# Up products of the gated feed-forward: high and low tokens in one 512-column product, halves added on VectorE, first tap and gate product on GpSimd

## The chip, the cores and the metric

One core of one Trainium2 chip runs the whole program: a four-layer network on 256 tokens of width 1024, all in float32. The metric is the device time of one execution in microseconds, the median of several runs. Before the change it is 1380.42 us (three runs, 1379.06 to 1381.10).

## The reference, cut to what matters

Two mixture-of-experts layers come first, then two layers (2 and 3 in the kernel) whose feed-forward part is this:

```python
def conv_ffn(h, w_in, conv_w, conv_b, w_out):
    """Gated MLP: up-projection -> causal depthwise conv (width 3) -> SiLU gate -> down-projection."""
    u = h @ w_in
    C = u.shape[-1]
    u = lax.conv_general_dilated(u, conv_w[:, None, :], window_strides=(1,),
                                 padding=[(CONV_WIDTH - 1, 0)],
                                 dimension_numbers=('NWC', 'WIO', 'NWC'),
                                 feature_group_count=C) + conv_b
    a, b = jnp.split(u, 2, axis=-1)
    return (jax.nn.silu(a) * b) @ w_out
```

`h` is 256 x 1024, `w_in` 1024 x 5632, so a and b have 2816 columns each, and `w_out` is 2816 x 1024. For each column, token t gets `w2*u[t] + w1*u[t-1] + w0*u[t-2] + bias`.

## The kernel before, in words

**Precision by parts.** TensorE takes the rounded type float32r. A float32 matrix is split into a high part, rounded by a copy (ScalarE, `copy`, line 793), and a low part, the raw value less the high one (VectorE). A product is three: high weights by high tokens, high weights by low tokens, low weights by high tokens, summed in one PSUM bank. `split_product` (lines 1857 to 1859) does these three for each of 8 k-blocks of 128 rows, each a 128x128 weight load and a product of 256 columns (the tokens).

**Steps and blocks.** The up projection runs in 11 steps of 256 columns of a and 256 of b. A step has two blocks (c = 0, 1) of 128 columns of a (ab = 0) and of b (ab = 1). Steps are called j = 0, 1 within five turns (four turns in a hardware loop, the fifth written out), and a last one, `step(2, None)`. A block's raw weights come by DMA in slots `Fa`, `Fb` (1 MB each, one pair per step, SyncE's queue, started when the `split` count shows an older slot done). The split weights lie in `w_high[c]`, `w_low[c]`, one buffer for each c: while TensorE makes block c of a step, the other buffer is refilled.

**The order on each engine, per step.** It is written out by hand; each engine goes through its list in order.
- TensorE (`feed_forward`, lines 2341 to 2351): block 0, block 1; each half waits for its weights' `split` count, and each block for its bank (banks 2j + c) to be free. Both halves of a block lie in one bank, 256 columns each. The first block of a layer is made in `next_x` by `passes` (line 1869) with the same products in another order.
- ScalarE (`step`, from line 1110): when a block is in its bank, it makes the high parts of the next step's weights for that buffer (`split_ffn`: two copies of 128x1024), then reads the bank twice for the affine start of the convolution, `w2*u + bias` into `F["conv"]` (line 1123), which sets `conv_begun`. After both blocks come two SiLU (line 1128), each waiting for `conv_done`.
- VectorE (`step`, from line 1655): two tiny copies of the taps (lines 1664, 1665); then for each block the two low parts of the next weights (line 1635), the tap of the token before for both halves (line 1676), and the tap of two tokens before (line 1681), both reading PSUM; at the end the two gate products (line 1694) into `F["gT"]`.
- GpSimd: nothing within the stage. Its queue issues the norms' gain and bias rows (`norm_rows`).

In the last step the weights split are the first of `w_out` (`split_down` on ScalarE, `low_down` on VectorE, lines 1644 and 1646), and with them the high and low parts of the gated tokens `g_high`, `g_low`. The down projection follows in 11 units; a unit is 24 products of 512 columns (lines 2366 to 2370), and unit i + 2 needs the buffers of unit i.

## Time and profile before

| | us |
|---|---|
| median of 3 runs | 1380.42 |
| profiled execution, whole | 1381.08 |
| profiled execution, span | 1379.3 |
| TensorE busy | 1309.4 |
| VectorE busy | 776.9 |
| ScalarE busy | 563.9 |
| GpSimd busy | 109.4 |
| layer 2, up stage: about | 891 to 1018 |
| layer 3, up stage: about | 1184 to 1309 |

Times in the rows are counted from the start of the span. A matmul's duration reaches beyond the start of the next one, since they overlap; the distance from start to start is what the stream costs. PE is TensorE, PEld its weight loads, DVE VectorE, ACT ScalarE, POOL GpSimd. `arena` is one large buffer in which `conv`, `gate`, `gT` and others lie, `bank` is PSUM, `slot` raw weights. In a row "x2" merges two operations in a line, and its duration is from the start of the first to the end of the second. "idle before <-releaser" is the idle time ahead of it and what ended it.

### The profile page before, as it was taken

Reading aid. Unit: us, or ns where it says so; the run is one execution under the profiler, and the core shown is the slowest. Engines: PE = TensorE matmul, PEld = TensorE weight load, DVE = VectorE, ACT = ScalarE, POOL = GpSimd, SP = SyncE. Lnnn points to the kernel's source line nnn. Section 1 sums busy time; section 2 is a strip of 40 time slices with the busy share of each in tenths; the row PEclk is TensorE's granted clock in tenths of the full one; section 3 lists DMA queues with packets and bytes.
Section 4 is the critical chain, followed back from the end, with each engine's and each line's share of the span. In section 5 each row is a group of like instructions: output and inputs, shape, how many; then the busy total and the mean of one; then the engine's idle time right before and its main releaser. Section 6 shows DMA issues by size and latency. Waiting matters only on the chain.

```text
span 1379.3 us, 20721 instructions
## 1 busy us (share of the span) xinstructions
PE 1309.4 (95%) x8104; PEld 975.9 (71%) x8104; DVE 776.9 (56%) x1462; ACT 563.9 (41%) x1012; POOL 109.4 (8%) x130
## 2 busy tenths in 40 slices
PE   7989999999899999999989999999999988999997
PEld 7867444444686764344339988899998876999985
DVE  3976312112578651112145799877775676577766
ACT  4563211211446431111124335276654473466552
POOL 1030000000001200000002362000000011000000
PEclk9999999999999989999998999999999999999999
DMA  9338899999744579999997437685756520656630
GB/s 304 134 149 331 352 421 421 421 421 421 244 151 183 217 289 423 421 421 421 421 384 233 147 102 116 153 272 183 243 213 209 182 70 1 214 183 198 245 136 31
DMA packets 130072, 347.64 MB, mean 252 GB/s; under 512 B 10277, under 2 KB 86331, under 8 KB 105412
## 3 DMA queue, kind: packets, MB, share of 16 engines
q1 hardware_dynamic: 125232, 332.29, 63.9%
q0 software_dynamic: 3888, 13.55, 4.3%
q8 instruction: 59, 0.97, 0.3%
q10 hardware_dynamic: 868, 0.63, 0.1%
q14 instruction: 25, 0.20, 0.0%
HBM read 342.25 MB, written 4.19 MB: 251 GB/s over the span
## 4 chain that ended last, share of the span: by engine, by line
PE 70%; DVE 14%; DMA 7%; SPq 4%; ACT 2%; issue 2%; POOL 0%; DVEq 0%; ACTq 0%
PE bank L2032 12%; PE bank L1857 9%; PE bank L1858 8%; PE bank L1859 8%; PE bank L2043 6%; SPq L664 4%; DMA slot<-in_w_up 4%; PE bank L2366 3%; PE bank L2370 3%; PE bank L2368 3%; DMA slot<-in_ffn_w_in 2%; PE bank L1742 2%; PE bank L1808 2%; PE bank L1869 1%; DVE ln_stats L1190 1%
## 5 line engine op out<-in xcount | busy, mean ns | idle before, releaser
L1857 PE MATMUL bank<-x_high,w_high 128*128 128x256 f32 x1040 | 295.7, 284 | 0.0
L1858 PE MATMUL bank<-x_low,w_high 128*128 128x256 f32 x1040 | 294.4, 283 | 0.0
L1859 PE MATMUL bank<-x_high,w_low 128*128 128x256 f32 x1040 | 294.3, 283 | 0.0
L793 ACT ACTIVATE w_high<-slot 128x1024 fp32r<-128x1024 f32 x214 | 215.6, 1054 | 178.5 <-PE bank L1859 78.9
L2032 PE MATMUL bank<-slot,arena 128*64 128x512 f32 x976 | 223.0, 592 | 1.6 <-DMA slot<-in_w_up 1.6
L1857 PEld LDWEIGHTS bank<-x_high,w_high 128*128 128x128 f32 x1040 | 199.7, 192 | 1.8 <-issue 1.7
L1858 PEld LDWEIGHTS bank<-x_low,w_high 128*128 128x128 f32 x1040 | 199.8, 192 | 0.1
L1859 PEld LDWEIGHTS bank<-x_high,w_low 128*128 128x128 f32 x1040 | 199.7, 192 | 0.0
L2032 PEld LDWEIGHTS bank<-slot,arena 128*64 128x64 f32 x976 | 73.3, 137 | 142.5 <-issue 142.3
L1635 DVE TENSOR_TENSOR w_low<-slot,w_high 128x1024 fp32r<-128x1024 f32 x88 | 104.0, 1222 | 58.2 <-ACT w_high L793 58.2
L1456 DVE TENSOR_TENSOR arena<-arena,bank 128x512 f32<-128x512 f32 x16 | 11.0, 688 | 200.9 <-PE bank L2032 200.9
L2043 PE MATMUL bank<-slot,arena 128*64 128x512 f32 x480 | 113.4, 595 | 0.9
L793 ACT ACTIVATE arena<-bank 128x512 f32<-128x512 f32 (+7 forms) x118 | 55.4, 501 | 142.7 <-PE bank L2117 85.2
L1464 DVE SCALAR_TENSOR_TENSOR y_low<-bank,slot_gates,y_high 128x512 fp32r<-128x512 f32 x32 | 24.0, 751 | 139.5 <-ACT y_high L980 139.5
L1246 DVE TENSOR_TENSOR w_low<-slot,w_high 128x1024 fp32r<-128x1024 f32 x46 | 54.2, 1221 | 46.3 <-ACT w_high L793 46.0
L1644 DVE TENSOR_TENSOR w_low<-slot,w_high 128x1024 fp32r<-128x1024 f32 x44 | 51.9, 1222 | 43.0 <-ACT w_high L793 42.8
L2043 PEld LDWEIGHTS bank<-slot,arena 128*64 128x64 f32 x480 | 35.1, 137 | 57.8 <-issue 56.0
L966 ACT ACTIVATE arena<-bank 128x512 f32<-128x512 f32 x16 | 9.6, 597 | 151.6 <-PE bank L2032 151.6
L980 ACT ACTIVATE y_high<-bank,slot_gates 128x512 fp32r<-128x512 f32 x32 | 22.0, 687 | 91.5 <-PE bank L2043 91.5
L2366 PE MATMUL bank<-w_high,g_high 128*128 128x512 f32 x176 | 55.7, 390 | 3.0 <-DVE g_low L1646 3.0
L2370 PE MATMUL bank<-w_high,g_low 128*128 128x512 f32 x176 | 55.5, 389 | 0.0
L2368 PE MATMUL bank<-w_low,g_high 128*128 128x512 f32 x176 | 55.5, 389 | 0.0
(345 smaller groups left out, 2196.9 us busy)
## 6 DMA issues: line engine op xcount, KB each, us to landing
slot<-in_w_gate SPq DMA_DIRECT2D x62, 1024.0 KB, 19.6
slot<-in_w_up SPq DMA_DIRECT2D x60, 1024.0 KB, 19.0
slot<-in_w_down SPq DMA_DIRECT2D x60, 1024.0 KB, 18.7
slot<-in_ffn_w_in SPq DMA_DIRECT2D x44, 1024.0 KB, 7.5
slot<-in_ffn_w_out SPq DMA_DIRECT2D x22, 1024.0 KB, 5.0
slot<-in_hgrn_w_in SPq DMA_DIRECT2D x16, 1024.0 KB, 6.7
slot<-in_w_in SPq DMA_DIRECT2D x10, 1024.0 KB, 9.8
slot<-in_w_o SPq DMA_DIRECT2D x8, 1024.0 KB, 4.9
```

Of the source, the lines that this page charges most:

```text
L664: sp.dma_start(slot(u, k, n), rows_of(name, src, k)).then_inc(slot_full[u.place], 16)
L793: return nc.scalar.activation(dst, src, ACT.Copy)
L1246: V.tensor_tensor(w_low[n % 2][:, ab, :, :], raw[:, :, P * ab:P * (ab + 1)], w_high[n % 2][:, ab, :, :].bitcast(F32), ALU.subtract)\
L1635: V.tensor_tensor(w_low[c][:, ab, :, :], raw[:, :, P * c:P * (c + 1)], w_high[c][:, ab, :, :].bitcast(F32), ALU.subtract)\
L1857: mm(dst, high[:, k, :], x_high[:, k, :], start=(k == 0), stop=False)
L1858: mm(dst, high[:, k, :], x_low[:, k, :], start=False, stop=False)
L1859: last = mm(dst, low[:, k, :], x_high[:, k, :], start=False, stop=(k == KD - 1))
L2032: last = mm(banks_gu["gu".index(m)][rows, :], xe[:, 4 * half + c, rows], ws[e][:, c, :], start=(half == 0 and c == 0), stop=(half == 1 and ...
L2043: last = mm(out[rows, :], B["actT"][:, c, rows], slot(W[(l, f"w{e}{c // 2}{names}")], 2, 1024)[:, c % 2, 512 * h:512 * (h + 1)], start=(c ...
L2366: mm(bs[t][h][:, :], gh[:, k, tok(t)], high[:, k, 512 * h:512 * (h + 1)], start=first, stop=False)
L2368: mm(bs[t][h][:, :], gh[:, k, tok(t)], low[:, k, 512 * h:512 * (h + 1)], start=False, stop=False)
L2370: last = mm(bs[t][h][:, :], gl[:, k, tok(t)], high[:, k, 512 * h:512 * (h + 1)], start=False, stop=final)
```

## The change

The high and low tokens lie side by side in one buffer `x_both`, so that one product of 512 columns takes high weights by both. It puts high-by-high into the first 256 columns of a bank and high-by-low into the last 256; the product with the low weights adds to the first. Each half of a block has its own bank now (8 in the loop). Only the first block of each layer keeps three narrow passes for each half.

ScalarE copies the low part out of PSUM (`rest`), then VectorE adds it to the other (`whole`, in SBUF). The affine start of the convolution moves from ScalarE to GpSimd and reads `whole`; both taps read `whole` too; the gate product moves from VectorE to GpSimd.

```diff
@@ -280,14 +280,16 @@
             load((l, f"F{n}{j}"), ("split", 2 * (FFN_UNIT[l] + 2 * (j + 1)), 8))
             body.append(order.pop())
         for c in range(2):
-            job(l, f"U{j}{c}", bank=2 * j + c)
+            for ab in range(2):
+                job(l, f"U{j}{c}{ab}", bank=4 * j + 2 * c + ab)
...
     for c in range(2):
-        job(l, f"U2{c}", bank=c)
+        for ab in range(2):
+            job(l, f"U2{c}{ab}", bank=2 * c + ab)
@@ -343,8 +345,8 @@
 
-        x_high = sb("x_high", [P, KD, T], F32R)
-        x_low = sb("x_low", [P, KD, T], F32R)
+        x_both = sb("x_both", [P, KD, 2, T], F32R)
+        x_high, x_low = x_both[:, :, 0, :], x_both[:, :, 1, :]
         w_high = [sb(f"w_high{c}", [P, 2, KD, P], F32R) for c in range(2)]
         w_low = [sb(f"w_low{c}", [P, 2, KD, P], F32R) for c in range(2)]
         x_tok = sb("x_tok", [P, NT, D])
@@ -468,7 +470,7 @@
         C["O"] = C["Q"].rearrange("p h t -> p (h t)").rearrange("p (t n) -> p t n", t=NT)
         C["O2"] = C["K"].rearrange("p h t -> p (h t)").rearrange("p (t n) -> p t n", t=NT)
 
-        F = carve([("gT", GC, T), ("conv", 4, T), ("gate", 2, T), ("cw_rows", 2, P), ("cw", 4, CH), ("cws", 2, 16), ("bias", SWQ, NK)])
+        F = carve([("gT", GC, T), ("conv", 4, T), ("gate", 2, T), ("cw_rows", 2, P), ("cw", 4, CH), ("cws", 2, 16), ("bias", SWQ, NK), ("whole", 4, T), ("rest", 4, T)])
         G = carve([("qT", 8, T), ("kraw", 2, T), ("kR", SWKV, T), ("v", NT, T), ("prob", 6, NK)])
         G["bias"] = F["bias"]
         early = xT[:, :, :].rearrange("p c t -> p (c t)")
@@ -775,10 +777,41 @@
                 src = bass.AP(skew.tensor, P - 1 + o, [[SWQ * NK - 1, P], [NK, SWQ], [1, KEYS[t]]])
                 pool.dma_start(F["bias"][:, :, K0[t]:K0[t] + KEYS[t]], src).then_inc(sem("skew_in"), 16)
             norm_rows(5, io["ln_ffn_g_2"][0], io["ln_ffn_b_2"][0])
+
+            def feed_forward(l):
+                def step(j, i):
+                    base = (l - 2) * STEPS + (STEPS - 1 if i is None else j)
+                    more = 0 if i is None else 2 * i
+                    w = F["cws"][:, j % 2, :].rearrange("p (k a c) -> p k a c", k=4, a=2)
+                    pool.wait_ge(sem("taps"), base + 1 + more)
+                    if base + more:
+                        pool.wait_ge(sem("gated"), 2 * (base + more))
+                    for c in range(2):
+                        for ab in range(2):
+                            evacuated(pool, (l, f"U{j}{c}{ab}"), i)
+                            last = nc.gpsimd.tensor_scalar(F["conv"][:, 2 * c + ab, :], F["whole"][:, 2 * c + ab, :],
+                                                           w[:, 2, ab, c:c + 1], w[:, 3, ab, c:c + 1], ALU.mult, ALU.add)
+                        last.then_inc(sem("conv_begun"), 1)
+                    for c in range(2):
+                        pool.wait_ge(sem("gate_done"), 2 * base + c + 1 + 2 * more)
+                        pool.wait_ge(sem("up_done"), 2 * base + c + 1 + 2 * more)
+                        if i is None:
+                            g = F["gT"][:, GC - 2 + c, :]
+                        else:
+                            g = F["gT"][:, 4 * i + 2 * j + c, :]
+                        nc.gpsimd.tensor_tensor(g, F["gate"][:, c, :], F["conv"][:, 2 * c + 1, :], ALU.mult).then_inc(sem("gated"), 1)
+
+                for i in range(STEPS // 2):
+                    step(0, i)
+                    step(1, i)
+                step(2, None)
+
+            feed_forward(2)
             norm_rows(6, io["ln_mix_g_2"][1], io["ln_mix_b_2"][1])
             conv_rows(1, F["cw_rows"])
             normalise(3, SWQ, G["prob"])
             norm_rows(7, io["ln_ffn_g_2"][1], io["ln_ffn_b_2"][1])
+            feed_forward(3)
 
 
         @block.scalar
@@ -1111,18 +1144,14 @@
                     base = (l - 2) * STEPS + (STEPS - 1 if i is None else j)
                     more = 0 if i is None else 2 * i
                     for c in range(2):
-                        b = produced(act, (l, f"U{j}{c}"), i)
+                        for ab in range(2):
+                            b = produced(act, (l, f"U{j}{c}{ab}"), i)
+                            last = copy(F["rest"][:, 2 * c + ab, :], b[:, T:2 * T])
+                        last.then_inc(sem("rest_ready"), 1)
                         if following:
                             split_ffn(l, *following, c)
                         else:
                             split_down(l, c)
-                        if c == 0:
-                            act.wait_ge(sem("taps"), base + 1 + more)
-                        for ab in range(2):
-                            w = F["cws"][:, j % 2, :].rearrange("p (k a c) -> p k a c", k=4, a=2)
-                            last = nc.scalar.activation(F["conv"][:, 2 * c + ab, :], b[:, T * ab:T * (ab + 1)], ACT.Identity,
-                                                        bias=w[:, 3, ab, c:c + 1], scale=w[:, 2, ab, c:c + 1])
-                        last.then_inc(sem("conv_begun"), 1)
                     for c in range(2):
                         act.wait_ge(sem("conv_done"), 2 * base + c + 1 + 2 * more)
                         nc.scalar.activation(F["gate"][:, c, :], F["conv"][:, 2 * c, :], ACT.Silu).then_inc(sem("gate_done"), 1)
@@ -1665,33 +1694,24 @@
                     V.tensor_scalar(w[:, :, 1, :], src(1), 1.0, None, ALU.mult).then_inc(sem("taps"), 1)
                     dve.wait_ge(sem("taps"), base + 1 + more)
                     for c in range(2):
-                        b = produced(dve, (l, f"U{j}{c}"), i)
+                        dve.wait_ge(sem("rest_ready"), 2 * base + c + 1 + 2 * more)
+                        for ab in range(2):
+                            b = produced(dve, (l, f"U{j}{c}{ab}"), i)
+                            drained(V.tensor_tensor(F["whole"][:, 2 * c + ab, :], b[:, 0:T], F["rest"][:, 2 * c + ab, :], ALU.add), (l, f"U{j}{c}{ab}"))
                         if following:
                             split_ffn(l, *following, c)
                         else:
                             low_down(l, c)
                         dve.wait_ge(sem("conv_begun"), 2 * base + c + 1 + 2 * more)
                         for ab in range(2):
-                            y, x = F["conv"][:, 2 * c + ab, :], b[:, T * ab:T * (ab + 1)]
+                            y, x = F["conv"][:, 2 * c + ab, :], F["whole"][:, 2 * c + ab, :]
                             last = V.scalar_tensor_tensor(y[:, 1:T], x[:, 0:T - 1], w[:, 1, ab, c:c + 1], y[:, 1:T], ALU.mult, ALU.add)
                         last.then_inc(sem("tap_done"), 1)
                         dve.wait_ge(sem("tap_done"), 2 * base + c + 1 + 2 * more)
                         for ab in range(2):
-                            y, x = F["conv"][:, 2 * c + ab, :], b[:, T * ab:T * (ab + 1)]
-                            last = V.scalar_tensor_tensor(y[:, 2:T], x[:, 0:T - 2], w[:, 0, ab, c:c + 1], y[:, 2:T], ALU.mult, ALU.add)
-                            if ab == 0:
-                                last.then_inc(sem("conv_done"), 1)
-                        drained(last, (l, f"U{j}{c}"))
-                    for c in range(2):
-                        dve.wait_ge(sem("gate_done"), 2 * base + c + 1 + 2 * more)
-                        if c == 0:
-                            evacuated(dve, (l, f"U{j}0"), i)
-                            evacuated(dve, (l, f"U{j}1"), i)
-                        if i is None:
-                            g = F["gT"][:, GC - 2 + c, :]
-                        else:
-                            g = F["gT"][:, bass.ds(4 * i + (2 * j + c), 1), :].rearrange("p o n -> p (o n)")
-                        V.tensor_tensor(g, F["gate"][:, c, :], F["conv"][:, 2 * c + 1, :], ALU.mult).then_inc(sem("gated"), 1)
+                            y, x = F["conv"][:, 2 * c + ab, :], F["whole"][:, 2 * c + ab, :]
+                            V.scalar_tensor_tensor(y[:, 2:T], x[:, 0:T - 2], w[:, 0, ab, c:c + 1], y[:, 2:T], ALU.mult, ALU.add)\
+                                .then_inc(sem(("conv_done", "up_done")[ab]), 1)
 
                 with dve.Fori(0, STEPS // 2 - 1) as i:
                     step(0, i, (1, i))
@@ -1858,6 +1878,17 @@
                     mm(dst, high[:, k, :], x_low[:, k, :], start=False, stop=False)
                     last = mm(dst, low[:, k, :], x_high[:, k, :], start=False, stop=(k == KD - 1))
                 return last
+
+            def wide_product(dst, high, low):
+
+                for k in range(KD):
+                    last = k == KD - 1
+                    if last:
+                        mm(dst[:, 0:T], low[:, k, :], x_high[:, k, :], start=False, stop=False)
+                    ins = mm(dst[:, :].rearrange("p (s n) -> p s n", s=2), high[:, k, :], x_both[:, k, :, :], start=(k == 0), stop=last)
+                    if not last:
+                        mm(dst[:, 0:T], low[:, k, :], x_high[:, k, :], start=False, stop=False)
+                return ins
 
             def passes(dst, n, ab, kinds, t=None, first=False, last=False):
 
@@ -2323,30 +2354,31 @@
                 for i in range(2):
                     last = nc.tensor.transpose(b[:, 88 * i:88 * (i + 1)], (conv_taps if l == DEPTH else F["cw_rows"])[0:88, i, :], ident[0:88, 0:88])
                 done(last, (l, "cw"))
-                b = reuse(pe, (l, "U00"), 0)
                 pe.wait_ge(sem("x_high_ready"), before_x + 4)
                 for ab in range(2):
+                    b = reuse(pe, (l, f"U00{ab}"), 0)
                     pe.wait_ge(sem("split"), 2 * n + ab + 1)
-                    passes(b, n, ab, "hw", first=True)
+                    for k in range(KD):
+                        mm(b[:, 0:T], w_high[0][:, ab, k, :], x_high[:, k, :], start=(k == 0), stop=False)
+                        mm(b[:, 0:T], w_low[0][:, ab, k, :], x_high[:, k, :], start=False, stop=(k == KD - 1))
                     if ab == 0:
                         transposes_out(l, y)
-                    last = passes(b, n, ab, "x", last=True)
-                done(last, (l, "U00"))
-                b = reuse(pe, (l, "U01"), 0)
+                    for k in range(KD):
+                        last = mm(b[:, T:2 * T], w_high[0][:, ab, k, :], x_low[:, k, :], start=(k == 0), stop=(k == KD - 1))
+                    done(last, (l, f"U00{ab}"))
                 for ab in range(2):
+                    b = reuse(pe, (l, f"U01{ab}"), 0)
                     pe.wait_ge(sem("split"), 2 * (n + 1) + ab + 1)
-                    last = split_product(b[:, T * ab:T * (ab + 1)], w_high[1][:, ab, :, :], w_low[1][:, ab, :, :])
-                done(last, (l, "U01"))
+                    done(wide_product(b, w_high[1][:, ab, :, :], w_low[1][:, ab, :, :]), (l, f"U01{ab}"))
 
             def feed_forward(l):
                 def step(j, i):
                     for c in range(2):
                         before_ = 2 * (FFN_UNIT[l] + c + (2 * STEPS - 2 if i is None else 2 * j)) + (0 if i is None else 8 * i)
-                        b = reuse(pe, (l, f"U{j}{c}"), i)
                         for ab in range(2):
+                            b = reuse(pe, (l, f"U{j}{c}{ab}"), i)
                             pe.wait_ge(sem("split"), before_ + (ab + 1))
-                            last = split_product(b[:, T * ab:T * (ab + 1)], w_high[c][:, ab, :, :], w_low[c][:, ab, :, :])
-                        done(last, (l, f"U{j}{c}"))
+                            done(wide_product(b, w_high[c][:, ab, :, :], w_low[c][:, ab, :, :]), (l, f"U{j}{c}{ab}"))
 
                 step(1, 0)
                 with pe.Fori(1, STEPS // 2) as i:
```

## Rows read from the trace of the kernel before

**Rows 1.** The page, part 1: busy time, share of the span and instructions.
```profile
PE 1309.4 (95%) x8104; PEld 975.9 (71%) x8104; DVE 776.9 (56%) x1462; ACT 563.9 (41%) x1012; POOL 109.4 (8%) x130
```

**Rows 2.** Table by stretch, up stages: length, busy per engine, PEclk, DMA share, GB/s.
```profile
893.00:1018.00 125.00, 125.00 (x1044) 125.00 (x1043) 95.75 (x171) 79.80 (x113) 2.25 (x3) 1.00 0.69 233
1205.00:1310.00 105.00, 105.00 (x875) 104.87 (x874) 81.44 (x146) 68.04 (x98) 0.00 (x0) 1.00 0.61 205
```

**Rows 3.** Timeline of TensorE, up stage of layer 2: start, duration, operation.
```profile
1001.02 0.28 PE L1857 MATMUL bank<-x_high,w_high 128*128 128x256 f32 x1
1001.14 0.28 PE L1858 MATMUL bank<-x_low,w_high 128*128 128x256 f32 x1
```

**Rows 4.** Timeline of TensorE, down stage of layer 2.
```profile
1021.14 0.62 PE L2368 MATMUL bank<-w_low,g_high 128*128 128x512 f32 x2
...
1022.50 0.62 PE L2368 MATMUL bank<-w_low,g_high 128*128 128x512 f32 x2
```

**Rows 5.** Timeline of ScalarE around the end of a loop turn.
```profile
937.50 2.01 ACT L793 ACTIVATE w_high<-slot 128x1024 fp32r<-128x1024 f32 x2 [2.75 <-PE bank L1859]
...
942.28 0.42 ACT L1128 ACTIVATE arena<-arena 128x256 f32<-128x256 f32 x1 [1.56 <-DVE arena L1681]
943.32 1.28 ACT L793 ACT_TABLE_LOAD   x1 [0.62 <-PE bank L1859]
...
946.53 1.00 ACT L1123 ACTIVATE arena<-bank,arena 128x256 f32<-128x256 f32 x2
```

**Rows 6.** Timeline of VectorE, the same block.
```profile
938.59 2.36 DVE L1635 TENSOR_TENSOR w_low<-slot,w_high 128x1024 fp32r<-128x1024 f32 x2 [1.61 <-ACT w_high L793]
940.87 0.87 DVE L1676 SCALAR_TENSOR_TENSOR arena<-bank,arena 128x255 f32<-128x255 f32 x2
941.77 0.87 DVE L1681 SCALAR_TENSOR_TENSOR arena<-bank,arena 128x254 f32<-128x254 f32 x2
```

**Rows 7.** Timeline of VectorE, layer 0: an operation of PSUM and SBUF.
```profile
94.38 0.42 DVE L1264 TENSOR_TENSOR x_low<-bank,x_high 128x256 fp32r<-128x256 f32 x1
94.72 0.17 DVE L1223 RECIPROCAL rinv<-rowsum 128x4 f32<-128x4 f32 x1
```

**Rows 8.** Timeline of VectorE, gate products and what follows.
```profile
1303.32 0.76 DVE L1694 TENSOR_TENSOR arena<-arena 128x256 f32<-128x256 f32 x2
1303.99 0.17 DVE L1664 TENSOR_SCALAR arena<-arena 128x8 f32<-128x8 f32 x1
```

**Rows 9.** GpSimd by form (busy us, mean ns, idle before), then L768 min/median/max ns.
```profile
L757 POOL MEMSET arena<- 128x2048 f32 x1 | 1.8, 1815 | 0.0
L731 POOL TENSOR_TENSOR arena<-arena,rinv 128x256 f32<-128x256 f32 x24 | 14.7, 611 | 187.0 <-DVE rinv L1223 187.0
L768 POOL TENSOR_TENSOR arena<-arena x14: 1060/1405/3234, 781.1 to 838.9; 128x512 f32<-128x512 f32 x14
```

**Rows 10.** Timelines of VectorE and of GpSimd in the recurrence of layer 2.
```profile
778.96 0.69 DVE L1583 TENSOR_TENSOR arena<-arena 128x512 f32<-128x512 f32 x1
779.56 2.02 DVE L1584 TENSOR_TENSOR arena<-arena 128x512 f32<-128x512 f32 x1
781.50 4.51 DVE L1538 TENSOR_TENSOR w_low<-slot,w_high 128x1024 fp32r<-128x1024 f32 x2
...
779.13 1.90 POOL L767 TENSOR_TENSOR arena<-arena 128x512 f32<-128x512 f32 x1 [45.22 <-DVE arena L1584]
782.44 2.50 POOL L767 TENSOR_TENSOR arena<-arena 128x512 f32<-128x512 f32 x1
```

**Rows 11.** Timelines of VectorE and of GpSimd, softmax of layer 0.
```profile
82.91 0.42 DVE L1214 CUSTOM_DVE_ANT_0 arena<-bank,tables 128x256 f32<-128x256 f32 x1
...
96.17 0.42 DVE L1214 CUSTOM_DVE_ANT_0 arena<-bank,arena 128x256 f32<-128x256 f32 x1
...
94.97 1.61 POOL L731 TENSOR_TENSOR arena<-arena,rinv 128x256 f32<-128x256 f32 x2 [0.95 <-DVE rinv L1223]
```

**Rows 12.** Timeline of VectorE: low tokens of the third down unit.
```profile
1027.28 0.68 DVE L1646 TENSOR_TENSOR g_low<-arena,g_high 128x512 fp32r<-128x512 f32 x1
```

## The prediction

> **What bounds the kernel now.** I read the page first: TensorE is busy 95% of the span at nearly full clock [rows 1]. Then the table by stretch, over the up stage of each layer: TensorE 125.00 of 125.00 us and 105.00 of 105.00 us, clock 1.00, VectorE 77%, ScalarE 64%, GpSimd nearly nothing, DMA 0.61 to 0.69 [rows 2]. In the list of waits for that stretch TensorE has no line; only the others wait, for its banks and for each other. So today the stage lasts what TensorE's stream lasts. The timeline gives its step: each 256-column product starts 0.12 us after the one in front [rows 3]; 512 columns take 1.36 us for six, 0.227 us each [rows 4]. A block (one c, both halves a and b) is 48 products of 0.12 us = 5.76 us, a step of two blocks is 11.52 us, and a layer has 11 steps.
>
> The others have room, but how much depends on the order of their queues. One loop turn is shown for ScalarE and VectorE [rows 5, 6]. Per block VectorE has two low halves of the weights (2.28 us, start to next start), four taps (0.90 + 0.87 us), and per step two gate products and two tiny tap copies: about 8.9 of 11.52 us.
>
> **What the change takes from TensorE.** 8 k-blocks of 3 x 0.120 = 0.360 us become 0.227 + 0.120 = 0.347 us; the columns are the same, one product's fixed share goes. Per layer 44 half-blocks less the first two (they keep three narrow passes) = 42, so 2 x 42 x 8 x 0.0127 = 8.5 us for the kernel, if TensorE stays the bound. A step would then take 32 x 0.3473 = 11.11 us.
>
> **What it puts on the others, and in which order.** ScalarE: four affine reads of PSUM per step (0.55 us, 0.45 apart) become four plain copies of the low part. They cost the same, but they now stand ahead of the weight copies, and VectorE can't touch a block before them. VectorE: gains four additions (one PSUM, one SBUF input, 256 columns: 0.42 us, next start 0.34 later [rows 7]), loses two gate products, and its taps read SBUF: I take the SBUF form's 0.34 us to the next start and 0.42 to a visible end, from the gate product today [rows 8], so the four taps last 0.34 + 0.42 + 0.02 + 0.34 + 0.34 = 1.46 us and `conv_done` comes after 1.20. GpSimd: gains per step four affine operations on 128x256 and two products on 128x256. The trace has no such affine operation. Bounds: a fill of 128x2048 takes 1.81 us, by proportion 0.23 us for 256 columns; a two-input product on 128x256 0.61 us, on 128x512 1.06 to 3.23 (median 1.4), so at most 0.8 [rows 9]. I take 0.50, just under the two-input 128x256 to which it is nearest, and 0.60 for the gate product.
>
> **The cost that decides: VectorE and GpSimd side by side.** In the recurrence both work on SBUF. VectorE's product of two SBUF tiles takes 0.69 us alone; the next of its kind, begun at 779.56 while GpSimd's (779.13 to 781.03) runs, takes 2.02 and ends 0.55 after GpSimd's end. The two low halves behind it take 4.51 us in place of 2.36, and GpSimd's, begun inside, 2.50 in place of some 1.3 [rows 10]. They alternate; neither shares. With one of VectorE's inputs in PSUM it isn't so: the score operation of 0.42 us lasts as long at 96.17 beside a GpSimd pair (94.97 to 96.58) as at 82.91 with none [rows 11]. The Trainium skill ("SBUF — State Buffer", section "Who interferes with whom") states that a VectorE instruction with two SBUF inputs and a GpSimd instruction that reads SBUF exclude each other for the whole instruction; by that rule, the trace agrees. Today GpSimd is idle in the stage and the taps have one input in PSUM. After the change low halves and taps have two SBUF inputs, and every GpSimd operation reads SBUF. So most GpSimd operations are added to VectorE's time.
>
> **The step, worked out.** I follow VectorE from one visible `conv_done` of block 1 to the next.
> (a) Between steps. The gate's SiLU starts 0.04 later and takes 0.42; then ScalarE copies the rest of block 0 (0.45 + 0.55; it could not do so before the SiLU, which is ahead of it), and VectorE starts 0.07 later: 1.53 us. In the loop the first step of a turn also has a table load of 1.28 ahead of its first copy [rows 5]: 2.81. The GpSimd gate product of block 1 falls in here, free.
> (b) Block 0, from the start of its first addition. First GpSimd operation 0.49 to 0.99. The first high half is ready at 0.93 (ScalarE starts it with the second copy's slot end, VectorE follows 1.10 after [rows 5, 6]); GpSimd runs until 0.99. Low half, GpSimd's second (0.50), low half: 0.99 + 1.14 + 0.50 + 1.14 = 3.77; the other order gives the same. Taps to 5.23.
> (c) Block 1 (copies ready long before). Additions 5.23 to 5.91; GpSimd 5.72 to 6.22 holds back the low half to 6.22; low to 7.36, GpSimd to 7.86, low to 9.00; the gate product of block 0, waiting since 7.86, to 9.60; `conv_done` at 10.80.
> Step: 12.33 us, 13.61 with the table load. Without exclusion (b) and (c) are 8.83, the steps 10.36 and 11.64, and TensorE's 11.11 would be the bound.
> Per layer there are ten intervals between eleven steps, three with the load (the loop's first turn finds ScalarE idle, the last is outside the loop): 3 x 13.61 + 7 x 12.33 = 127.1 against 10 x 11.52 = 115.2: +11.9. In: the first step's block 1 ends about 1.0 later (GpSimd adds 1.4, TensorE is 0.4 earlier). Out: down unit 2 has its tokens' low part at 1027.96 today [rows 12] and TensorE reaches it at 1017.94 + 2 x 24 x 0.2273 = 1028.85, so 0.9 is absorbed. About +12.0 a layer, +24 in all. TensorE idles 1 to 2.4 us between blocks; I price no clock loss, since a half-clock stretch would fall into that idle time.
> The profiled execution took 1381.1 (span 1379.3, 1.8 around it): 1405; its median is 0.7 lower: **1404 us**.
>
> With GpSimd at 0.30 in place of 0.50 the first operation of a block hides and the same sum gives +8; at 0.23 about +4; at 0.60 +32; at 0.80 about +50. For the range the ends are +4 and +50.
> The Trainium skill ("GPSIMD Engine Reference", "3.1 Elementwise — side-by-side cycle accounting") gives 1.8 cycles an element at best for one input and 2.6 for two, at 1.2 GHz; as an estimate from it, 0.38 and 0.55 us, and the sum would be +13. The measured 0.61 us stands a little above its two-input figure.
>
> **What costs nothing.** The interleaved x_high/x_low changes only strides: each product still reads 256 or 512 adjacent columns. Eight banks in the loop in place of four: a bank comes back after two steps, drained by the addition long before. The down products' banks 4 to 7 were drained a step earlier. New waits for `rest_ready`: behind VectorE's wait stands only that block's work, counted in (a). GpSimd's queue: behind the first feed-forward stands the next norm's rows, which waited for a norm after it anyway; ahead of it stand only this norm's rows, issued while TensorE makes the first block. Weight loads are no bound: the DMA engines are 0.69 and 0.61 busy over the stage [rows 2], with the same bytes after.
>
> **Rivals.**
> A, no exclusion for this pair (affine operations have one SBUF input, the measured ones had two; or VectorE goes first and GpSimd waits where nobody cares). Then TensorE stays the bound: 1380.4 - 8.5 = 1372. It decides as soon as VectorE's step is under 11.11 us, that is if GpSimd adds under 0.4 us to a step's 10.7 (mean of 10.36 and 11.64, three in ten). For it: slack today. Against: [rows 10] show both engines stretched. 15%.
> B, GpSimd slower than its rows: strides, two per-partition scalars and the alternation put an affine operation at 0.8 us or above: 4 x 0.3 more a step, +50: 1430. For it: up to 3.2 us for 128x512 in the recurrence. Against: the strides here are plain. 10%.
> C, the wide product doesn't gain (a narrow one behind a wide one waits for its weights) and no exclusion: TensorE keeps 11.52, the time stays at 1380. 4%. With exclusion C changes nothing, since TensorE is no longer the bound.
> D, partial exclusion: collisions half as costly, +3 to +5: 1384. 5%.
>
> **How the numbers follow.** Forecast (1385 to 1425) 66%, A 15%, B 10%, D 5%, C 4%. A measurement of this kernel tells 0.2% (2.8 us) from no change. Faster: A and a share of C, 0.17. Same: most of C and the edge of D, 0.05. Slower: the rest, 0.78. The range goes from 1377 (A left out) to 1430, about 80%.
>
> **What would show it.** Right: up stage of layer 2 at some 137 us from first to last product in place of 127; TensorE idle before the first product of a block, released by `w_low`; low halves (1.22 us today) with a mean over 1.5; GpSimd operations that begin inside a low half twice their shortest. (a) right: VectorE idle 1 us per step ahead of the first addition, released by ScalarE. Wrong, if `w_low` stays at 1.22 us and TensorE without idle time: then A. If the pitch wide to narrow isn't 0.227 + 0.120, the first part is wrong. If GpSimd's affine shortest is over 0.7 us, B.

## The result and the profile after

The changed kernel takes 1401.14 us (median of four runs, 1398.87 to 1405.16) against 1379.74 for the kernel before: ratio 1.0159, 95% interval 1.0132 to 1.0186. It is slower by 21.4 us; 1404 was forecast.

First the groups of the page (busy us, mean ns, idle before it), as far as they answer to [rows 1], [rows 6] and [rows 9]:

```profile
PE 1307.6 (93%) x7432; PEld 938.2 (67%) x7432; DVE 811.1 (58%) x1506; ACT 546.7 (39%) x1012; POOL 279.6 (20%) x262
L1888 PE MATMUL bank<-x_both,w_high 128*128 128x512 f32 x672 | 236.9, 403 | 14.5 <-DVE w_low L1664 14.5
L792 POOL TENSOR_SCALAR arena<-arena 128x256 f32<-128x256 f32 x88 | 138.3, 1580 | 79.3 <-DVE arena L1700 79.3
L1664 DVE TENSOR_TENSOR w_low<-slot,w_high 128x1024 fp32r<-128x1024 f32 x88 | 110.5, 1296 | 9.2 <-ACT w_high L826 7.1
```

TensorE now waits for the low halves (14.5 us in all). GpSimd's affine operation has a mean of 1.58 us. The view of that line shows that this is not what it takes by itself (min/median/max in ns):

```profile
L792 POOL TENSOR_SCALAR arena<-arena x88: 551/1624/3092, 896.0 to 1332.0; 128x256 f32<-128x256 f32 x88
```

The table by stretch, for both up stages, answers to [rows 2]: the columns are the window and its length, then busy us and count of PE, PEld, DVE, ACT and POOL, the granted clock, the DMA share and GB/s. TensorE, which had no gaps before, is busy 92 to 93% of it.

```profile
893.00:1028.00 135.00, 124.15 (x691) 106.37 (x690) 109.93 (x187) 72.39 (x116) 80.84 (x65) 0.99 0.63 211
1205.00:1330.00 125.00, 115.93 (x637) 99.02 (x636) 105.03 (x180) 68.55 (x111) 76.50 (x59) 0.98 0.56 188
```

One step with a table load on VectorE's timeline (start, duration), which answers to [rows 6]:

```profile
934.84 0.76 DVE L1700 TENSOR_TENSOR arena<-bank,arena 128x256 f32<-128x256 f32 x2 [0.57 <-ACT arena L826]
935.70 2.53 DVE L1664 TENSOR_TENSOR w_low<-slot,w_high 128x1024 fp32r<-128x1024 f32 x2
938.61 0.88 DVE L1708 SCALAR_TENSOR_TENSOR arena<-arena 128x255 f32<-128x255 f32 x2 [0.38 <-POOL arena L792]
939.53 0.88 DVE L1713 SCALAR_TENSOR_TENSOR arena<-arena 128x254 f32<-128x254 f32 x2
940.32 0.75 DVE L1700 TENSOR_TENSOR arena<-bank,arena 128x256 f32<-128x256 f32 x2
940.99 2.55 DVE L1664 TENSOR_TENSOR w_low<-slot,w_high 128x1024 fp32r<-128x1024 f32 x2
944.00 1.34 DVE L1708 SCALAR_TENSOR_TENSOR arena<-arena 128x255 f32<-128x255 f32 x2 [0.46 <-POOL arena L792]
945.38 0.88 DVE L1713 SCALAR_TENSOR_TENSOR arena<-arena 128x254 f32<-128x254 f32 x2
...
948.40 0.76 DVE L1700 TENSOR_TENSOR arena<-bank,arena 128x256 f32<-128x256 f32 x2 [2.00 <-ACT arena L826]
...
960.55 0.76 DVE L1700 TENSOR_TENSOR arena<-bank,arena 128x256 f32<-128x256 f32 x2 [0.57 <-ACT arena L826]
```

And GpSimd in the same time, with VectorE's first low half by itself:

```profile
935.47 0.56 POOL L792 TENSOR_SCALAR arena<-arena 128x256 f32<-128x256 f32 x1 [0.47 <-DVE arena L1700]
936.01 2.57 POOL L792 TENSOR_SCALAR arena<-arena 128x256 f32<-128x256 f32 x1
940.84 1.63 POOL L792 TENSOR_SCALAR arena<-arena 128x256 f32<-128x256 f32 x1 [2.26 <-DVE arena L1700]
943.93 0.73 POOL L802 TENSOR_TENSOR arena<-arena 128x256 f32<-128x256 f32 x1
...
935.70 1.40 DVE L1664 TENSOR_TENSOR w_low<-slot,w_high 128x1024 fp32r<-128x1024 f32 x1
```

To be seen: the first affine operation, alone, takes 0.56 us. The low half that starts inside it takes 1.40 us, not 1.22. The second affine operation starts at 936.01, inside that low half, sits through both low halves (to 938.23) and ends at 938.58, after 2.57 us. The taps wait for it (0.38 us idle). In block 1 the gate product (943.93 to 944.66) stretches the tap pair from 0.88 to 1.34. Steps: 13.56 us with a table load (934.84 to 948.40), 12.15 without (948.40 to 960.55). Nearly all the other steps of both layers take 12.1 or 13.6 us too; one in layer 2 takes 15.11 (907.60 to 922.71).

The measure that varies least from execution to execution (185.7 us in both layers of e1, e7 and e9) is the length of a layer's feed-forward, from the start of the first up product to the start of the last down product. Before: 188.2 us in both layers. After: 201.4 and 199.7. That is +24.6 us; the rest of this profiled execution was 4.1 us shorter than in the one before, though its work is the same. Over all the profiled executions of this study layer 2's first up product starts at 886.5 to 893.1 us, although the program ahead of it is the same in all. So a few us of every single total are not the stage's. Much of that goes with TensorE's granted clock, which falls to its lower level (1.2 GHz) for stretches of 3.4 to 10.2 us. In the twelve profiled executions the part outside the two feed-forwards has 36.4 to 63.6 us of such stretches and takes 996.6 to 1005.7 us, the two with a correlation of 0.91 (52.6 us in the kernel before, 43.1 in the changed one). The medians show it as well: of 13 executions of the kernel before, run beside e9 and e10, the one with a mean granted clock of 0.987 took 1374.74 us and the four with 0.980 took 1379.99 to 1381.70.

### The profile page after: what moved, and what is told of

The parts are those of the page before. It is cut to its first block, busy times and chain, and to the rows that moved or that the text cites. A ratio compares the mean times of both kernels' runs of the same rounds, so it can differ in the third digit from the quotient of the medians.

```text
span 1399.8 us, 19609 instructions
## 1 busy us (share of the span) xinstructions
PE 1307.6 (93%) x7432; PEld 938.2 (67%) x7432; DVE 811.1 (58%) x1506; ACT 546.7 (39%) x1012; POOL 279.6 (20%) x262
## 4 chain that ended last, share of the span: by engine, by line
PE 48%; DVE 22%; DMA 8%; POOL 7%; issue 6%; SPq 4%; ACT 3%; DVEq 0%; ACTq 0%; POOLq 0%
PE bank L2063 11%; POOL arena L792 7%; PE bank L2074 6%; SPq L666 4%; DMA slot<-in_w_up 4%; DMA slot<-in_ffn_w_in 4%; DVE arena L1708 3%; PE bank L2398 2%; PE bank L1877 2%; PE bank L2402 2%; PE bank L1879 2%; PE bank L2400 2%; PE bank L1878 2%; PE bank L1828 2%; DVE arena L1713 1%
## 5 line engine op out<-in xcount | busy, mean ns | idle before, releaser
L1888 PE MATMUL bank<-x_both,w_high 128*128 128x512 f32 x672 | 236.9, 403 | 14.5 <-DVE w_low L1664 14.5
L1890 PE MATMUL bank<-x_both,w_low 128*128 128x256 f32 x588 | 166.2, 283 | 0.0
L792 POOL TENSOR_SCALAR arena<-arena 128x256 f32<-128x256 f32 x88 | 138.3, 1580 | 79.3 <-DVE arena L1700 79.3
L1888 PEld LDWEIGHTS bank<-x_both,w_high 128*128 128x128 f32 x672 | 123.1, 190 | 42.0 <-DVE w_low L1664 16.9
L826 ACT ACTIVATE arena<-bank 128x256 f32<-128x256 f32 (+6 forms) x206 | 85.0, 449 | 161.6 <-PE bank L2148 85.0
L1664 DVE TENSOR_TENSOR w_low<-slot,w_high 128x1024 fp32r<-128x1024 f32 x88 | 110.5, 1296 | 9.2 <-ACT w_high L826 7.1
L1890 PEld LDWEIGHTS bank<-x_both,w_low 128*128 128x128 f32 x588 | 112.5, 191 | 3.0
L1877 PE MATMUL bank<-x_both,w_high 128*128 128x256 f32 x368 | 105.2, 286 | 0.0
L1878 PE MATMUL bank<-x_both,w_high 128*128 128x256 f32 x368 | 104.1, 283 | 0.0
L1879 PE MATMUL bank<-x_both,w_low 128*128 128x256 f32 x368 | 104.1, 283 | 0.0
L1275 DVE TENSOR_TENSOR w_low<-slot,w_high 128x1024 fp32r<-128x1024 f32 x46 | 54.2, 1222 | 45.0 <-ACT w_high L826 44.6
L733 POOL TENSOR_TENSOR arena<-arena,rinv 128x256 f32<-128x256 f32 (+1 forms) x48 | 38.6, 825 | 187.5 <-DVE rinv L1252 187.5
L1673 DVE TENSOR_TENSOR w_low<-slot,w_high 128x1024 fp32r<-128x1024 f32 x44 | 52.6, 1237 | 40.3 <-ACT w_high L826 40.1
L1877 PEld LDWEIGHTS bank<-x_both,w_high 128*128 128x128 f32 x368 | 70.6, 192 | 1.7 <-issue 1.7
L1878 PEld LDWEIGHTS bank<-x_both,w_high 128*128 128x128 f32 x368 | 70.6, 192 | 0.1
```

The source lines that it names most:

```text
L792: last = nc.gpsimd.tensor_scalar(F["conv"][:, 2 * c + ab, :], F["whole"][:, 2 * c + ab, :], w[:, 2, ab, c:c + 1], w[:, 3, ab, c:c + 1], AL ...
L826: return nc.scalar.activation(dst, src, ACT.Copy)
L1275: V.tensor_tensor(w_low[n % 2][:, ab, :, :], raw[:, :, P * ab:P * (ab + 1)], w_high[n % 2][:, ab, :, :].bitcast(F32), ALU.subtract)\
L1664: V.tensor_tensor(w_low[c][:, ab, :, :], raw[:, :, P * c:P * (c + 1)], w_high[c][:, ab, :, :].bitcast(F32), ALU.subtract)\
L1877: mm(dst, high[:, k, :], x_high[:, k, :], start=(k == 0), stop=False)
L1878: mm(dst, high[:, k, :], x_low[:, k, :], start=False, stop=False)
```

## The experiments

Ratios are to the kernel before, on the same chips. "FF" is the length defined above, layer 2 and layer 3.

| | median us | ratio, 95% | FF us |
|---|---|---|---|
| e1_both_back | 1373.68 | 0.9960 (0.9943 to 0.9977) | 185.7, 185.7 |
| e2_gate_back | 1401.72 | 1.0160 (1.0141 to 1.0180) | 200.2, 198.5 |
| e3_affine_fill | 1378.82 | 0.9995 (0.9984 to 1.0007) | 186.4, 186.4 |
| e4_narrow | 1404.63 | 1.0187 (1.0165 to 1.0209) | 201.2, 199.9 |
| e5_both_back_narrow | 1380.68 | 1.0009 (0.9997 to 1.0021) | 188.3, 188.3 |
| e6_beside_reads | 1384.99 | 1.0043 (1.0027 to 1.0060) | 190.1, 189.6 |
| e7_beside_fills | 1373.98 | 0.9960 (0.9945 to 0.9974) | 185.7, 185.7 |
| e8_grouped | 1372.67 | 0.9952 (0.9939 to 0.9964) | 185.8, 184.6 |
| e9_fill_gate_back | 1373.93 | 0.9969 (0.9956 to 0.9983) | 185.7, 185.7 |
| e10_third_affine | 1426.17 | 1.0340 (1.0318 to 1.0362) | 211.8, 211.3 |

**e1: both GpSimd parts go back.**

```diff
-  nc.gpsimd.tensor_scalar(conv, whole, w2, bias, mult, add)        # GpSimd
+  nc.scalar.activation(conv, whole, Identity, bias=bias, scale=w2) # ScalarE
-  nc.gpsimd.tensor_tensor(g, gate, conv_b, mult)                   # GpSimd
+  V.tensor_tensor(g, gate, conv_b, mult)                           # VectorE
```

> The wide product, the copy of the low part on ScalarE and the addition on VectorE stay; the affine start goes back to ScalarE (it reads the sum in SBUF) and the gate product back to VectorE. Theory (GpSimd's reads exclude VectorE's two-input operations, and that alone makes VectorE's step longer than TensorE's): GpSimd idle, low halves 1.22 us again, VectorE's step 12.15 - 0.84 (idle ahead of the taps) - 0.46 (stretched tap) - 0.2 = about 10.6 us, 11.9 with a table load; mean of ten 11.0, so TensorE's 11.11 us is the bound: 1372 to 1375 us. Rival (the detour itself, copy then addition ahead of the weight splits, is what lengthens the step): 1390 us or more.

As the theory said: 1373.68 us. TensorE has no wait between the first up and the first down product. The copy and the addition stayed, so the detour through SBUF is not what costs; and the wide product pays here.

**e2: only the gate product goes back** (the second half of e1's edit).

> Only the gate product goes back to VectorE; the affine start stays on GpSimd. Theory: the tap stretched by 0.46 us once per step is gone, the gate product of block 0 no longer stands between; the two products cost VectorE 0.7 us but fall into its idle time while ScalarE copies. 20 steps x 0.5 = 10 us less than the changed kernel: about 1391 us. Rival (handshakes with GpSimd, not what it does): half of the loss goes with a third of the operations, about 1394 and the tap's stretch stays.

Both missed: no gain in the median, 2.3 us in the two FF lengths. (In this execution the first products of layer 2's down stage ran at the lower clock level, 0.50 from 1026.2 to 1033, and that stage took 64.4 us, against 62.9 in the changed kernel, so the 2.3 us is rather too small.) VectorE's steps are 12.30 us and 13.19 with a table load, where the changed kernel has 12.14 and 13.57. The stretched tap is gone (0.88 again), but look at the end of a step on VectorE:

```profile
958.67 0.88 DVE L1704 SCALAR_TENSOR_TENSOR arena<-arena 128x254 f32<-128x254 f32 x2
959.77 0.76 DVE L1714 TENSOR_TENSOR arena<-arena 128x256 f32 x2 [0.23 <-ACT arena L1148]
960.45 0.17 DVE L1684 TENSOR_SCALAR arena<-arena 128x8 f32 x1
960.52 0.17 DVE L1685 TENSOR_SCALAR arena<-arena 128x8 f32 x1
960.90 0.76 DVE L1691 TENSOR_TENSOR arena<-bank,arena 128x256 f32<-128x256 f32 x2 [0.21 <-DVE arena L1685]
```

The gate products wait for ScalarE's SiLU and then stand ahead of the tap copies and the next additions: from the visible `conv_done` (959.15) to the next addition 1.75 us, where the changed kernel needs 1.12. I had called that time idle and free; it isn't long enough once the SiLU is taken off. The gate product costs about the same on either engine here.

**e3: a fill in place of the affine operation.**

```diff
-  last = nc.gpsimd.tensor_scalar(conv, whole, w2, bias, mult, add)
+  last = pool.memset(conv, 0.5)
```

> GpSimd fills the conv tile with a constant in place of reading the sum (the affine start is left out of the result); every wait and signal stays, the gate product stays on GpSimd. A fill reads no SBUF. Theory: the fills run beside VectorE's low halves, 0.25 to 0.35 us each, low halves 1.22 us, VectorE no longer idle ahead of the taps of either block; left is the gate product's collision (0.5 to 0.7 us a step). Step 12.15 - 0.84 - 0.2 = 11.1 us, 12.4 with a table load, against TensorE's 11.11: 1379 to 1384 us. Rival (the round trip over GpSimd's queue and semaphores costs, whatever it does): 1395 us or more, with the idle time ahead of the taps still there.

1378.82 us, 0.2 below the theory's range and far from the rival's. The fills take 0.31 us each, and every low half that meets only fills keeps its length (27 of them, 1.21 to 1.23 us). The theory missed where the gate product would fall: it now meets low halves as well as taps. Twelve low halves take up to 1.77 us, each beside a gate product, and the mean is 1.30. Two blocks, each VectorE and then GpSimd, the first with fills and the second with a gate product as well:

```profile
957.46 2.36 DVE L1663 TENSOR_TENSOR w_low<-slot,w_high 128x1024 fp32r<-128x1024 f32 x2
957.17 0.56 POOL L792 MEMSET arena<- 128x256 f32 x2 [0.42 <-DVE arena L1699]
...
939.08 2.90 DVE L1663 TENSOR_TENSOR w_low<-slot,w_high 128x1024 fp32r<-128x1024 f32 x2
939.97 0.93 POOL L801 TENSOR_TENSOR arena<-arena 128x256 f32<-128x256 f32 x1 [0.43 <-ACT arena L1156]
```

Chain, queue and semaphores are the changed kernel's, so they are not the cost. What is left against e1 is 1.4 us by the FF lengths (186.4 against 185.7, twice); the medians differ by 5.1, so the rest of that difference is not the stage's.

**e4: three narrow products again, all else as changed.**

```diff
-  mm(dst[:, 0:512], high[k], x_both[k], ...); mm(dst[:, 0:256], low[k], x_high[k], ...)
+  mm(dst[:, 256:512], high[k], x_low[k], ...)          # for all k first
+  mm(dst[:, 0:256], high[k], x_high[k], ...); mm(dst[:, 0:256], low[k], x_high[k], ...)
```

> The wide product is replaced by three products of 256 columns into the same two halves of the bank; everything else is the changed kernel's. TensorE's step goes from 11.11 back to 11.52 us. Theory (VectorE with GpSimd sets the step, 12.15 to 13.57 us, TensorE waits): 1401 to 1403 us, the gain of 8.5 us was never seen. Rival (TensorE is still on the path, its idle time only shifts): 1409 us.

FF lengths 201.2 and 199.9 against 201.4 and 199.7: TensorE's part of the change had no effect in the changed kernel. VectorE's steps agree as well: 12.15 and 13.58 us, there 12.14 and 13.57. The median lies 3.5 us above the changed kernel's, less than the rival's 8 and with overlapping runs (1399.47 to 1406.22 against 1398.87 to 1405.16).

**e5: e1 with narrow products** (edit of e4).

> e1_both_back with the wide product replaced by three of 256 columns. TensorE's step is 11.52 us again, and in e1_both_back TensorE is never idle in the stage. Theory (there the product's form is worth its full difference, 8 x 0.0075 = 0.06 us a half block as the starts in e1 show, 84 half blocks): 5 us slower than e1_both_back, 1378 to 1380 us. Rival (e1 gained through something else, for instance the banks or the copies): 1374 us, as e1.

1380.68 us and FF 188.3, the length before. So with TensorE as the bound the wide form is worth 2 x 2.6 = 5.1 us, and that is all that e1 gains.

**e6 and e7: GpSimd works beside e1, and nobody waits for it.** After each addition one operation into an unused tile.

```diff
+  evacuated(pool, (l, f"U{j}{c}{ab}"), i)
+  nc.gpsimd.tensor_scalar(spare, constant_tile, s0, s1, mult, add)   # e6: reads SBUF
+  pool.memset(spare, 0.5)                                            # e7: only writes
```

> e1_both_back with GpSimd operations that nobody waits for: after each addition one affine operation on 128x256 that reads a constant tile in SBUF and writes an unused one (88 in all, as many as in the changed kernel). Theory (a GpSimd read of SBUF holds VectorE's two-input operations): VectorE's step of about 11.1 to 11.7 us grows by 0.2 to 0.56 us for each of four operations, TensorE begins to wait: 1380 to 1394 us, the taps or low halves stretched in the trace. Rival (only the waits on GpSimd cost): 1374 us, as e1_both_back.

> As e6_beside_reads, but the 88 operations are fills of the same 128x256 tile: they read no SBUF. Theory (reads exclude): nothing is stretched, 1374 us, low halves 1.22 us. Rival (any GpSimd work on SBUF holds VectorE up): slower than e1_both_back by half of what e6 loses or more.

The groups and the lines of the low halves and of the first tap (min/median/max), e6 first, then e7:

```profile
L796 POOL TENSOR_SCALAR arena<-rep,gnorm 128x256 f32<-128x256 f32 x88 | 138.1, 1570 | 121.9 <-DVE arena L1703 107.2 <-POOL arena L796 7.6 <-issue 7.1
L1667 DVE TENSOR_TENSOR w_low<-slot,w_high x88: 1210/1222/1440, 870.8 to 1304.1; 128x1024 fp32r<-128x1024 f32 x88
L1711 DVE SCALAR_TENSOR_TENSOR arena<-arena x88: 471/482/704, 900.5 to 1318.4; 128x255 f32<-128x255 f32 x88
```

```profile
L796 POOL MEMSET arena<- 128x256 f32 x88 | 27.5, 313 | 216.9 <-DVE arena L1703 204.6 <-issue 7.1
L1667 DVE TENSOR_TENSOR w_low<-slot,w_high x88: 1214/1220/1227, 870.0 to 1294.6; 128x1024 fp32r<-128x1024 f32 x88
L1711 DVE SCALAR_TENSOR_TENSOR arena<-arena x88: 476/479/485, 900.1 to 1308.0; 128x255 f32<-128x255 f32 x88
```

The same affine operation on another tile has the same mean, 1.57 us, and the kernel loses 11 us against e1 (8.3 by the FF lengths) although nothing depends on it. The fill has 0.31 us and costs nothing: 40 low halves meet one, and all take 1.21 to 1.23 us. This is the separation: reading, not presence, and not a wait. The two operations also differ in kind and in length (0.56 us alone against 0.31); a write-only operation as long as the affine one was not run.

**e8: the wide products of a half block together.**

```diff
-  for k: wide(k); narrow(k)
+  for k in 0..6: wide(k)
+  for k in 0..7: narrow(k)
+  wide(7)
```

> e1_both_back with the same 16 products of a half block in another order: seven wide, then the eight narrow, then the last wide, instead of in turn. In e1 a half block takes 2.82 us, eight pairs of 0.3525, where 0.2273 + 0.120 = 0.3473 was forecast from rows of streams of one size. Theory G (the alternation of sizes costs the 0.005 us a pair): 2.78 us a half block, 84 x 0.04 = 3.4 us less, 1370 us, which would be the fastest version. Rival (a wide product of this kind just takes 0.2325): no change, 1374 us.

The starts on TensorE, e8 and then e1 (first row of a half block and of the next):

```profile
986.40 2.00 PE L1872 MATMUL bank<-x_both,w_high 128*128 128x512 f32 x8
988.24 1.11 PE L1877 MATMUL bank<-x_both,w_low 128*128 128x256 f32 x8
989.20 2.00 PE L1872 MATMUL bank<-x_both,w_high 128*128 128x512 f32 x8
```

```profile
986.08 0.63 PE L1875 MATMUL bank<-x_both,w_high 128*128 128x512 f32 x2
...
988.90 0.63 PE L1875 MATMUL bank<-x_both,w_high 128*128 128x512 f32 x2
```

Eight wide in a row take 1.84 us, 0.230 each, eight narrow 0.96. A half block takes 2.80 in place of 2.82 us, not 2.78: theory G holds for half of it at best. FF gains nothing in layer 2, where TensorE waits once (0.75 us, for a low half), and 1.1 us in layer 3; against e1 the median is 1 us lower with overlapping runs. e8 and e1 both beat the kernel before and the changed one; between them this doesn't decide.

**e9: fill, and the gate product on VectorE.**

> The changed kernel with GpSimd's affine replaced by a fill (the affine start is left out of the result) and the gate product back on VectorE. GpSimd keeps its place in the chain, with every wait and signal, but reads no SBUF in the stage at all. Theory (all of the loss is reads against two-input operations): TensorE never waits, low halves 1.22 us, 1373 to 1376 us, like e1_both_back. Rival (the gate product on VectorE, which gained nothing in e2, costs as much here): 1379 us or more.

1373.93 us, FF as e1. With no GpSimd operation that reads SBUF left in the stage, nothing of the loss is left, with GpSimd still in the middle of the chain. And the gate product costs VectorE nothing here, where it has slack.

**e10: a third affine operation per block.**

```diff
+  if ab == 1: last = nc.gpsimd.tensor_scalar(unused, whole_b, w2, bias, mult, add)
   last.then_inc(sem("conv_begun"), 1)
```

> The changed kernel with one more affine operation per block on GpSimd, ahead of the signal for the taps (it writes a tile that nobody reads). Alone it takes 0.56 us. Theory (VectorE's two low halves and GpSimd's operations run one after the other, and the taps wait for the last of them): 44 blocks x 0.56 us = 24 us more than the changed kernel, 1424 to 1427 us. Rival (GpSimd's operations beside the low halves cost their stretched 1.58 us each, whatever else runs): 44 x 1.5 = 66 us more, 1467 us.

```profile
L792 POOL TENSOR_SCALAR arena<-arena 128x256 f32<-128x256 f32 x88 | 139.2, 1591 | 74.6 <-DVE arena L1703 74.6
L795 POOL TENSOR_SCALAR arena<-arena 128x256 f32<-128x256 f32 x44 | 24.5, 556 | 0.0
```

25.0 us more than the changed kernel for 44 operations: 0.57 us each (0.50 by the FF lengths, 22.0 us; 0.54 by VectorE's steps, 13.23 us in place of 12.14), and the third shows 0.556, since no low half is left in front of it. Its 1.58 us siblings are 0.56 of work and the rest standing still.

## Why the prediction was right

Point by point, by its steps:

- **TensorE was the bound, the others had slack.** Right (e5 and e1: the products' form alone moves the time).
- **TensorE's gain, 8.5 us.** Mis-sized. The pair takes 0.3525 us, not 0.347: a wide product in this stream takes 0.230 to 0.2325, where the down stage's took 0.2273 [rows 4]. Where TensorE is the bound it is worth 5.1 us (e1 against e5). It didn't enter the forecast, as e4 shows.
- **VectorE and GpSimd exclude each other; the affine takes 0.50.** The mechanism is right, shown by e3, e6, e7 and e9, and the size was 0.56. The rule of the Trainium skill ("SBUF — State Buffer", section "Who interferes with whom") says the same of reads and of operations that only write; by that rule, e6's operations are held up and e7's are not, and the runs agree (1.57 against 0.31 us).
- **They alternate.** Half right. In block 1 they do (1.63 us for the first affine operation, which starts 0.15 us ahead of the low halves, 1.51 for the second). In block 0 the second affine operation waits through both low halves, so the standing still fell on GpSimd (median 1.62) and the low halves' mean went to 1.30 only. The sign that I named for VectorE, a mean over 1.5, was wrong; the one for GpSimd, twice its shortest, was right. The order doesn't change the sum, since the taps wait for whichever is last.
- **The pieces of a step.** (a) 1.12 us for 1.53, 2.54 for 2.81: two plain copies take 0.66 us, not the 1.00 of the affine reads [rows 5]. (b) 5.48 for 5.23 and (c) 5.54 for 5.57: taps on SBUF take 0.48 us, not 0.42, the gate product on GpSimd 0.74, not 0.60. Together 12.15 for 12.33, and 13.56 for 13.61. So the errors had different signs, and the step came out nearer than its parts deserved. That is luck: by the forecast's own figures for 0.50 and 0.60 us, an affine operation of 0.56 gives about +29 in place of +24, and the shorter (a), 0.41 us in 20 steps, takes 8 of it back.
- **Length of the stage.** From first to last up product some 137 us were forecast, 135.0 and 133.7 measured (126.7 before). TensorE idles 0.5 to 2.1 us at a time there, 1 to 2.4 were forecast. Then it waits 3.0 and 2.4 us for the first low tokens of the down stage, and that stage takes 62.9 and 63.1 us in place of 61.4. Both FF lengths together: +24.6 for +24.
- **Weight loads are no bound.** Right but for one step. ScalarE waits 2.26 us for raw weights at 908.42, and this is the step of 15.11 us, 1.5 of layer 2's 201.4. The kernel before has the same wait (1.80 us, until 911.66), and with TensorE as the bound it cost nothing.
- **No clock loss.** Right in sum, but not for the reason given. Before, the granted clock was 1.00 through both feed-forwards. In the changed kernel it falls to its lower level, 1.2 GHz, three times for 3.4 us, after TensorE has waited several times. Twice that is inside an up stage (977.8, 1278.2), where the steps keep their 12.14 and 13.57 us, as forecast. The third time it is in the first down unit of layer 3, where TensorE has no wait (columns as in the table by stretch):

```profile
1322.00:1329.00 7.00, 4.56 (x26) 3.72 (x25) 5.99 (x12) 6.20 (x11) 4.36 (x3) 1.00 0.79 300
1329.40:1332.80 3.40, 3.40 (x10) 2.62 (x9) 3.40 (x6) 0.42 (x1) 2.43 (x2) 0.50 0.63 255
```

Seven products there start 0.43 us apart, not 0.227. Layer 2's down stage has no such stretch but waits 0.91 us for the low tokens of its third unit, which layer 3's does not; so the two end up 0.2 us apart. In e4 the clock falls as often (948.3, 1275.9, 1327.1), so e4 doesn't test this.
- **Rival A** would have been right had GpSimd only written: that is e9. **Rival B**'s sign, a shortest over 0.7 us, didn't come (0.551). **C** fell with e5 (the wide form does gain, 5.1 us), **D** with the measured loss and e10.
- The rest of the program ran 4.1 us shorter in the profiled execution. It had 9.5 us less at the lower clock level (43.1 against 52.6), and by the line through all twelve (0.28 us for each of these) that is 2.7 of it. The rest, and what decides how often the clock falls there, no run here tests.

## What to carry to other kernels

An engine that is idle is not free capacity if its operations read what its neighbour's two-input operations read: here 132 operations, some 82 us of work on an idle GpSimd, made the two feed-forwards 29.7 us longer than e1's. Before moving work, list for each operation how many SBUF inputs it has, also for those that change their source (here the taps went from PSUM to SBUF). And look for the shortest instance of a stretched operation: the gap between minimum and median is time spent waiting for the neighbour.

## What the runs showed of the hardware

A 128x512 product with 128x128 weights starts 0.2273 us after the one in front in the down stage, but 0.230 in a row of eight of its kind here and about 0.2325 in alternation with 256-column ones (e8, e1); why is open. A plain ScalarE copy of 128x256 from PSUM goes at 0.66 us a pair, the affine read with scale and bias by pointer at 1.00. And when two low halves stand back to back on VectorE, the start of a GpSimd affine operation decides where it ends. In the five runs that have them (the changed kernel, e2, e4, e6, e10), all 88 that start within the first low half last until both are done (2.36 to 3.10 us). All 186 that start 0.14 to 0.26 us ahead of it end 0.27 us after the first low half at the latest (0.55 to 1.63 us). The 13 of e2 that start 0.05 us ahead also last until both are done (2.66 us). Why the limit lies there, no run here shows.
